# 448 tokens instead of 384 on the gathered path of a PEER layer, 640 instead of 704 on the dense one, and a down product turned round

## The reference, cut to what matters

```python
x = x + merged @ w_o                      # called x2 in the kernel
h2 = rms_norm(x, ffn_g)
x = x + peer(h2, w_q, s_keys, e_u, e_v)

def peer(h, w_query, sub_keys, expert_u, expert_v):      # per token t
    qry = (hb @ w_query).reshape(t, 8, 2, 128)
    s = einsum('thcd,hckd->thck', qry, sub_keys)
    top_s, top_i = top_k(s, 16)                          # per half
    cand_s, cand_i = sums and pairs of the two halves    # 256 per head
    best_s, best_pos = top_k(cand_s, 16)
    expert = take(cand_i, best_pos); gate = softmax(best_s)
    a = einsum('td,thkd->thk', hb, expert_u[expert])
    act = gelu(a) * gate
    return einsum('thk,thkd->td', act, expert_v[expert])
```

## Time and profile before

| | |
|---|---|
| median of three runs | 3921.18 us |
| profiled execution: its own time | 3919.27 us |
| its span, first to last instruction | 3917.3 us |
| TensorE busy (matmul) | 3506.5 us, 90% |
| VectorE busy | 2583.2 us, 66% |
| GpSimd busy | 1505.9 us, 38% |
| ScalarE busy | 1121.7 us, 29% |
| moved by DMA | 775.30 MB, mean 198 GB/s |

### The profile page before, as it was taken

How to read it: one execution, slowest core, us unless ns; L and a number is a source line. 1 busy time by engine, 2 the same in 40 slices (tenths; PEclk the granted TensorE clock), 3 DMA queues, 4 the chain that set the end, 5 groups by cost and what they waited for, 6 DMA issues and landing times.

```text
span 3917.3 us, 55124 instructions
## 1 busy us (share of the span) xinstructions
PE 3506.5 (90%) x20014; PEld 3179.2 (81%) x20014; DVE 2583.2 (66%) x5650; ACT 1121.7 (29%) x1642; POOL 1505.9 (38%) x1154
## 2 busy tenths in 40 slices
PE   7999987999979970566399999999999999999998
PEld 6888874566649860566399999999999999999998
DVE  3000004433316999899388878888888888888887
ACT  3111113333311110899222222222222222222221
POOL 0000004322200000000366666667766666666774
PEclk9999998999989995899699999999999999999999
DMA  3222225222240000355888888888888888888987
GB/s 132 92 91 91 91 81 194 95 105 86 68 150 26 16 7 5 100 165 156 279 293 294 293 285 288 292 291 316 311 303 295 291 293 289 289 288 286 324 307 259
DMA packets 335792, 775.30 MB, mean 198 GB/s; under 512 B 39088, under 2 KB 142512, under 8 KB 334256
## 3 DMA queue, kind: packets, MB, share of 16 engines
q0 software_dynamic: 110592, 402.70, 29.3%
q1 hardware_dynamic: 198160, 336.04, 26.2%
q10 hardware_dynamic: 26912, 35.13, 2.5%
HBM read 680.73 MB, written 93.06 MB: 198 GB/s over the span
## 4 chain that ended last, share of the span: by engine, by line
PE 47%; DMA 2%; DVE 1%; POOL 1%; issue 0%; ACT 0%; ACTq 0%; DVEq 0%
PE exp_vp L1835 24%; PE exp_up L1822 23%; DMA exp_ring<-in_v,exp_eid 1%; DMA exp_acc<-scratch_h2T 1%; DMA exp_ring<-in_u_rows,exp_eid 1%; POOL exp_v_lo L1602 0%; POOL exp_ring L1611 0%; DVE exp_am_lo L1724 0%; DVE exp_now L1749 0%; DVE exp_ring L1743 0%; DVE exp_acc L1731 0%; DMA exp_u_raw<-scratch_x 0%; DMA out_yp<-exp_u_raw 0%; DVE exp_acc L1711 0%; DVE exp_u_raw L1800 0%
## 5 line engine op out<-in xcount | busy, mean ns | idle before, releaser
L1822 PE MATMUL exp_up<-exp_h_hi,exp_u_hi 128*128 128x352 f32 x2048 | 661.4, 323 | 60.2 <-POOL exp_u_lo L1597 55.1
L1731 DVE TENSOR_TENSOR exp_acc<-exp_acc,exp_vp 128x352 f32<-128x352 f32 x1024 | 529.5, 517 | 256.6 <-PE exp_vp L1835 242.5
L1835 PE MATMUL exp_vp<-exp_am_hi,exp_v_hi 128*128 128x352 f32 x2048 | 660.9, 323 | 4.6 <-DVE exp_am_lo L1724 4.6
L1822 PE MATMUL exp_up<-exp_h_lo,exp_u_hi 128*128 128x352 f32 x2048 | 661.1, 323 | 0.0
L1835 PE MATMUL exp_vp<-exp_am_lo,exp_v_hi 128*128 128x352 f32 x2048 | 660.6, 323 | 0.0
L1822 PE MATMUL exp_up<-exp_h_hi,exp_u_lo 128*128 128x352 f32 x2048 | 660.4, 322 | 0.0
L1835 PE MATMUL exp_vp<-exp_am_hi,exp_v_lo 128*128 128x352 f32 x2048 | 659.6, 322 | 0.0
L1611 POOL DMA_INDIRECT exp_ring<-in_u_rows,exp_eid x384 | 367.1, 956 | 608.0 <-DMA exp_eid<-scratch_eid 321.5
L1749 DVE SCALAR_TENSOR_TENSOR exp_now<-exp_ring,exp_dot,exp_now 128x1024 f32<-128x1024 f32 x381 | 488.9, 1283 | 31.8 <-DMA exp_ring<-in_v,exp_eid 31.2
L1743 DVE CUSTOM_DVE_ANT_0 exp_ring<-exp_now,exp_ring 128x1024 f32<-128x1024 f32 x384 | 467.8, 1219 | 40.5 <-DMA exp_ring<-in_u_rows,exp_eid 39.5
L1611 POOL DMA_INDIRECT exp_ring<-in_v,exp_eid x384 | 365.3, 951 | 293.6 <-DVE exp_now L1749 232.9
(11 more groups left out here) (205 smaller groups left out, 5446.5 us busy)
## 6 DMA issues: line engine op xcount, KB each, us to landing
exp_u_raw<-in_u SPq DMA_DIRECT2D x128, 512.0 KB
exp_v_raw<-in_v SPq DMA_DIRECT2D x128, 512.0 KB
exp_gt<-scratch_gates SPq DMA_DIRECT2D x128, 352.0 KB
scratch_gates<-spr_g SPq DMA_DIRECT2D x5, 8192.0 KB
scratch_z<-prj_zo ACTq DMA_DIRECT2D x33, 768.0 KB, 3.5
prj_w_raw<-in_w_in SPq DMA_DIRECT2D x44, 512.0 KB, 4.4
mix_zg<-scratch_z SPq DMA_DIRECT2D x9, 1024.0 KB
rt_wq<-in_w_q SPq DMA_DIRECT2D x4, 2048.0 KB, 18.0
```

What stands on the lines that cost most here:

```text
L1731: V.tensor_tensor(acc[:, k, cols(g)], acc[:, k, cols(g)], vp[:, n % 4, 0:GW], ALU.add).then_inc(added, 1)
L1822: last = nc.tensor.matmul(up[:, g, 0:GW], u[a][:, o, k * P:(k + 1) * P], h2[b][:, k, cols(g)], start=(k == 0 and n == 0), stop=(k == KD - ...
L1835: last = nc.tensor.matmul(vp[:, m % 4, 0:GW], v[a][:, 2 * (1 - half) + o, k * P:(k + 1) * P], am[b][:, 1 - half, o, cols(g)], start=(o == ...
```

## The change

Sparse tokens become 448 (`N0` + 64 = `S0`), dense ones 640 (`TD`), five tiles of 128 (`NTD`), with `GW` = 320.

- The 64 extra sparse tokens make half a tile: they stand twice in the 128 partitions, and each copy takes half of the 128 picks, so this tile needs 64 fetches. A full pass is 448 picks with u and 448 with v, in eight phases: 64, 128, 128, 128 and again. Per step 14 picks on average, up to 15.
- In the down product the gated values are the stationary operand (128 tokens), v the moving one (512 features): 5 token tiles x 2 halves x 2 groups x 3 passes = 60 matmuls of 512 columns, in 10 parts (`ND`). The result is tokens by features, so `acc` starts as x2 itself and is stored as it is; the transposes and the last additions of x2 go, as does the clearing of `acc`. x2 (2.6 MB) is loaded into `acc` once h2 has been split.
- The ring has eight rows: the fetch of row n + 8 waits until row n is taken.
- VectorE has 10 places m; a table says how many picks stand at each (`BETWEEN`; `LATE` in the first step of a phase). GpSimd's groups of fetches in a step become 4, 3, 4 and the rest.
- The sparse tiles' h2 and x2 are loaded in turn into two buffers and their results are stored during the stage, from ScalarE's queue.
- `spread` writes five tiles of 128 tokens and none of 64. `route` writes `eid` and `gate` for four tiles, the fourth in part.

```diff
-TD = TOK - N0
-NTD = NT - NS
-GW = TD // 2
+HS = 64
+S0 = N0 + HS
+TD = TOK - S0
+NTD = TD // P
...
+    BETWEEN = (1, 1, 2, 1, 2, 1, 2, 1, 2, 2)
+    LATE = (0, 0, 2, 2, 2, 2, 2, 2, 2, 2)
+    HALVES = [(m + 1) * 8 // ND - m * 8 // ND for m in range(ND)]
...
+            sp.wait_ge(h2_lo_ready, KD)
+            sp.dma_start(acc[:, :, :], d["x2"][S0:TOK, :].rearrange("(t p) e -> p t e", p=P)).then_inc(acc_in, 16)
...
             for n in range(RING):
                 fetch(n)
             split_u(0)
             for q in range(NQ):
                 ahead = [n + RING for n in picks_of(q)]
                 split_u(2 * q + 1)
-                for n in ahead[0:3]:
+                for n in ahead[0:4]:
                     fetch(n)
                 split_v(2 * q)
-                for n in ahead[3:6]:
+                for n in ahead[4:7]:
                     fetch(n)
                 if q + 1 < NQ:
                     split_u(2 * q + 2)
-                for n in ahead[6:9]:
+                for n in ahead[7:11]:
                     fetch(n)
                 split_v(2 * q + 1)
-                for n in ahead[9:]:
+                for n in ahead[11:]:
                     fetch(n)
...
             def add(q, m):
-                n = NU * (q - 1) + m
-                g, k = m // KD, m % KD
+                n = ND * (q - 1) + m
+                t, c = m // 2, slice(m % 2 * 512, m % 2 * 512 + 512)
+                if n == 0:
+                    dve.wait_ge(acc_in, 16)
                 dve.wait_ge(down_ready, n + 1)
-                V.tensor_tensor(acc[:, k, cols(g)], acc[:, k, cols(g)], vp[:, n % 4, 0:GW], ALU.add).then_inc(added, 1)
+                V.tensor_tensor(acc[:, t, c], acc[:, t, c], vp[:, n % 4, :], ALU.add).then_inc(added, 1)
...
+            def down_part(q, half, m):
+
+                t, c = m // 2, slice(m % 2 * 512, m % 2 * 512 + 512)
+                bank = (2 * (1 - half) + m) % 4
+                if m == 0:
+                    pe.wait_ge(v_lo_ready, 2 * q)
+                    pe.wait_ge(am_lo_ready, 4 * q - 1)
+                if m == 4:
+                    pe.wait_ge(am_lo_ready, 4 * q)
+                after(pe, added, ND * (q - 1) + m - 3)
+                for o in range(2):
+                    for n, (a, b) in enumerate(passes):
+                        last = nc.tensor.matmul(vp[:, bank, :], am[b][:, 1 - half, o, t * P:t * P + P],
+                                                v[a][:, 2 * (1 - half) + o, c], start=(o == 0 and n == 0), stop=(o == 1 and n == 2))
+                last.then_inc(down_ready, 1)
...
-            pe.wait_ge(added, NU * NQ)
-            for t in range(NTD):
-                n = min(P, TD - t * P)
-                after(pe, y_ready, 2 * (t - 2) + 2)
-                for c in range(2):
-                    for k in range(4):
-                        last = nc.tensor.transpose(vp[0:n, 2 * (t % 2) + c, k * P:(k + 1) * P],
-                                                   acc[:, 4 * c + k, t * P:t * P + n], ident[:, :])
-                    last.then_inc(y_turned, 1)
```

More of the change, by code:

```diff
@@ L1128, in store @@
             def store(t):
-                if t < NS:
+                if t <= NS:
                     act.wait_ge(eid_ready, t + 1)
@@ L1701, in _ @@
             act.wait_ge(taken, 2 * PICKS)
-            nc.scalar.copy(own[:, NS - 1, :], now[:, :]).then_inc(now_out, 1)
+            nc.scalar.copy(own[:, (PHASES - 1) % 2, :], now[:, :]).then_inc(now_out, 1)
+            store(PHASES - 1)
+            act.wait_ge(own_stored, 16 * NP_)
         @block.vector
@@ new lines, in begin @@
+            def begin(p):
+                if p < NP_:
+                    dve.wait_ge(now_set, p + 1)
+                    return
+                if p == NP_:
+                    dve.wait_ge(half_zeroed, 1)
+                else:
+                    dve.wait_ge(now_out, p - NP_)
+                if p == NP_ + 1:
+                    V.tensor_tensor(own[0:HS, 0, :], own[0:HS, 0, :], now[0:HS, :], ALU.add).then_inc(half_ready, 1)
+                    dve.wait_ge(half_ready, 1)
+                dve.wait_ge(own_in[p % 2], own_loaded(p))
@@ L1803, in _, with up_half @@
         @block.tensor
         def _(pe):
-            pe.wait_ge(ident_in, 16)
             passes = ((0, 0), (0, 1), (1, 0))
+            def up_half(q, w):
+                o, g, part = w // 4, w // 2 % 2, w % 2
+                j = 2 * q + o
+                if part == 0:
+                    if g == 0:
+                        pe.wait_ge(u_lo_ready, j + 1)
+                    after(pe, prod_ready, NG * j + g - 1)
+                for k in range(4 * part, 4 * part + 4):
+                    if isinstance(q, int) and q == 0 and w < 2:
+                        pe.wait_ge(h2_lo_ready, k + 1)
+                    for n, (a, b) in enumerate(passes):
+                        last = nc.tensor.matmul(up[:, g, 0:GW], u[a][:, o, k * P:(k + 1) * P], h2[b][:, k, cols(g)],
+                                                start=(k == 0 and n == 0), stop=(k == KD - 1 and n == 2))
+                if part == 1:
+                    last.then_inc(up_ready, 1)
@@ L1839, in _ @@
+                        for _ in range(HALVES[m]):
+                            up_half(q, w)
+                            w += 1
+                    if down:
+                        down_part(q, half, m)
             step(0, 0, down=False)
```

279 lines of the change are left out of this document (130 added, 149 removed).

## The result

The changed kernel takes 3873.26 us (median of 4 runs, 3871.06 to 3876.0) against 3921.7 us of the kernel before on the same chip (four runs now, 3919.73 to 3923.97): a ratio of 0.9884, with a 95% interval of 0.9872 to 0.9896. It is faster by 1.2%, where 4.2% were forecast, and the time lies 38 us above the range.

The account below looks back on a forecast made before the run. TensorE bounds the kernel now; after the change the loop through VectorE and GpSimd would. 3919.3 - 128 (last stage) - 20.1 (`spread`) - 16.4 (tail) = 3754.8, with 1.9 for the runs 3757 us; range 3705 to 3835.

Parts of the forecast that it names:

- the tail: After the last down matmul: one add, one store and the close take 5.3 us instead of 21.7, 16.4 less.
- DMA allowance: Last stage: 0.15 us added to each step, 9.5 us in all, for rows that come late.
- the loop in the u phases: Last stage, u steps: the loop through VectorE and GpSimd takes 28.1 us, half a microsecond more than TensorE needs.
- The chain itself: Each step: add at 14.0, two picks, fetch, split_u at 20.7, four fetches to 25.6, split_v 28.0, TensorE 28.1 us; 55%.
- The v steps: Last stage, v phases: 28.3 us a step, 0.09 more for two slower picks and about as much for the wait behind.
- The turns of phase: First step of a phase: the 7th pick comes later; 3 us for each of 7 changes, 21 us, bounds 0.8 and 4.
- TensorE's clock: Last stage: matmul times at full clock; only the half-clock restart in step one costs, some 3 us.
- The ring of eight doesn't help here: Step loop: eight rows only give a row eight picks to land and remove VectorE waits (32 us) off the path.
- The start: Last stage: loads before the first matmul unchanged (-3 to +4 us); first up to first down 26 us, x2 load beside it.
- TensorE's own step: Last stage: 96 x 0.1464 + 60 x 0.2262 = 27.63 us; as rival, it alone sets the step, 3690 us, 12%.
- The DMA case: Rival, last stage: DMA engines set 29.6 us a step and rows come late; 3822 us, or 3795 with cheaper packets; 27%.
- `spread`: Stage before the last: five tile stores, none of 64 tokens; it ends at 1869.0 us, 20.1 us gained.

Follow-up runs that it names:

- experiment 1: Changed kernel with the product written back to PSUM and the low part reading it there, so with one SBUF operand: 3800.05 us, ratio 0.9694.
- experiment 2: Changed kernel with two of the four fetches between split_u and split_v moved behind split_v: 3768.69 us, ratio 0.9619.
- experiment 4: Changed kernel with the edits of experiment 1, experiment 2 and experiment 3 at once: 3715.09 us, ratio 0.9481.
- experiment 6: Changed kernel with a ring of four rows instead of eight, nothing else: 4135.51 us, ratio 1.0561.
- experiment 3: Changed kernel with the x2 load put behind the next load of u and v in SyncE's queue: 3866.18 us, ratio 0.9862.
- experiment 8: Kernel of experiment 4 with picks placed earlier in the first step of a phase (`LATE`): 3707.68 us, ratio 0.946 to the changed kernel.

## Why the prediction was wrong, by its steps

Against the forecast span the kernel lost 117 us: 0.7 and 5.7 gained ahead of the first up matmul, 0.2 lost in the tail, 123.5 between. These 123.5 are 10.2 from first up to first down, 82 in the 31 u steps (970.1 against 888 with their turns, restart and DMA allowance), 30 in the 32 v steps (952.8 against 922), and 0.8 in the last down product.

- **The failing step, the loop in the u phases.** "A product or low part of 320 columns 0.40 to 0.50" was the duration of an undisturbed one. The low part at place 3 is held to the end of the split_v beside it, 3.33 us in the step shown and in 25 of 31. So "VectorE begins that add at 14.0" failed too: in that step it is 16.5. Four fifths of what these phases lost goes with the hold: experiment 1 takes 67 of the 82 us away. The evidence stood in the profile before, a mean of 601 ns where a product has about 0.5 us. I sized the link by the earlier trace rows of an add and never listed the low part. A mean above the usual length of its kind asks for the long ones to be looked at, most of all where the instruction goes onto the path.
- **The chain itself was right.** Pick, fetch, split_u, four fetches, split_v, TensorE: experiment 2 cuts it and TensorE's step appears. With the hold away the ordinary u steps are 28.5 us, 0.4 above the 28.1 of the sum. One number beside it was wrong: split_u, four fetches and split_v are 9.7 us by the prediction's own lengths; the 11.1 us count from the end of the 7th pick and hold its fetch as well.
- **The v steps, 28.95 instead of 28.3.** Two v picks in a row take 2.59 us from start to the next start (3575.36 to 3577.95), 1.30 each where I had 1.19, and the fourth fetch is 0.26 us late by it:

```profile
3575.36 2.67 DVE L1795 SCALAR_TENSOR_TENSOR exp_now<-exp_ring,exp_dot,exp_now 128x1024 f32<-128x1024 f32 x2
...
3577.95 0.48 DVE L1752 TENSOR_TENSOR exp_pr<-exp_up,exp_gt 128x320 f32<-128x320 f32 x1
...
3578.97 0.94 POOL L1618 DMA_INDIRECT exp_ring<-in_v,exp_eid  x1 [0.30 <-issue]
...
3580.49 0.94 POOL L1618 DMA_INDIRECT exp_ring<-in_v,exp_eid  x1 [0.58 <-issue]
...
3581.45 2.40 POOL L1609 TENSOR_TENSOR exp_v_lo<-exp_v_raw,exp_v_hi 128x1024 fp32r<-128x1024 f32 x1
...
3584.08 0.49 PE L1870 MATMUL exp_vp<-exp_v_hi,exp_am_hi 128*128 128x512 f32 x1 [0.81 <-POOL exp_v_lo L1609]
```

  The pair that holds the 7th pick takes the same 2.6 us, 0.2 more than forecast. The earlier trace rows show a v pick ahead of an add, and no pair. The two delays are some 0.5 us of the 0.65 by which a step is longer; the rest of it wasn't followed. At 0.65 us a step they are 21 of the 30 us; what is left is in the turns and the steps behind them. Here low part and split_v just miss each other (in this step one ends at 3567.37 and the other begins at 3567.61), which is why experiment 1 leaves the v phases as they are.
- **The turns of phase, 3 us each with a bound of 4: too little.** In experiment 1, without the hold, a turn step is 3.2 us longer than its neighbours in the u phases, as worked out, and 3.0 to 4.6 in the v phases. But the step behind is longer as well, by 1.5 us at the first turn, at a mean granted clock of 0.94. All that the steps of experiment 1 behind the first take above their ordinary length is 43 us, some 6 for each of the seven turns.
- **TensorE's clock was put at nothing after the first step.** The forecast has every step at full clock. In the changed kernel the stage's matmuls are busy for 1828 us at 0.97, in experiment 4, where TensorE hardly waits, for 1793 us at 0.99. These 35 us are a part of the losses told above, not one beside them.
- **"The ring of eight doesn't help here": wrong.** The waits for rows of before were taken as the most that a ring of four could cost, and only the 32 us for rows of u were counted, not the 31 for rows of v. They belonged to a step of 30.66 us with 12 rows; with 14 rows a step and no cover, four rows cost 262 us (experiment 6). My number was right here only because the kernel has the ring. Had I priced the change without this part, I would have had to ask how long a row takes to land beside the picks that it has for it.
- **The start.** "The x2 load is needed a step later" was true of x2 and not of what stands behind it: SyncE issues the next u group's load after it, at 1890.96, it landed 23.6 us later by the chain of waits, and split_u stood for it. 10.2 us, and experiment 3 gives 9.8 back there. That the first up matmul came 5.7 us earlier than before, counted from the stage's begin, I had put at nothing; no run shows why.
- **TensorE's own step** is 27.83 us, not 27.63: in the stage a down matmul follows the one before after 231 ns (median), where the first stage had 226. Right within 1%.
- **The DMA case, 27%,** was priced too high: 29.6 us a step by the packet times of before, while no row was late in experiment 4 with steps of 27.8 us at 365 GB/s. The allowance of 9.5 us wasn't needed.
- **`spread` (1868.3 for 1869.0) and the tail (5.5 for 5.3)** came as worked out. TensorE's waits, though, were for 2.5 us in a u step and not 0.5.

What stays open: why x2 lands later in experiment 8, what of the v turns is ScalarE's copies of `now`, how deep the ring has to be between four and eight, and which of the steps with a wait get the lower clock.

## What to carry to other kernels

Before an instruction is put onto the path, list its group and compare mean and usual length: what is held by another engine costs nothing while it has cover, and much of its length when a change takes the cover away. Give the low part an operand in PSUM, or keep the other engine's long instruction away from it. And price each part of a change by its absence, too: a buffer that only "removes waits off the path" can be what keeps them off it. Count the clock with the waits: some of the steps in which TensorE stands, or which follow one, also have slower matmuls.

## What the runs showed of the hardware

- A VectorE instruction with two SBUF operands was held up to 3.33 us by a GpSimd split of 2.4 us, 70 of 256 times over 620 ns, and in 256 of 256 times not at all (484 ns) when one operand came from PSUM (experiment 1). No split was lengthened in turn (2.45 us at most).
- One core moved 363 to 367 GB/s in stretches of 400 us at a DMA share of 0.98, 106 of 146 MB of it rows fetched by index (experiment 4, 2400 to 2800 us), against 300 GB/s at 0.87 before.
- TensorE's mean granted clock over the last stage was 0.99 in experiment 4, where it hardly stood, 0.97 in the changed kernel with waits of 2.5 us a step, and 0.91 in experiment 6, where it stood again and again for up to 9.4 us. The same 9984 matmuls were busy for 1793, 1828 and 1924 us.
